# Last attention: first query slot alone, query low parts ahead of a weight's, three output slots side by side

## The chip, the core and the metric

The kernel runs on one core of a Trainium2 chip. The metric is the device time of one execution in microseconds (us), from the first to the last instruction with what lies around them; the median of several executions is given, and a profiled execution has its own time. All work is in fp32 that is split in two parts, as told below.

## The reference, cut to what matters

Four layers work on x of 512 tokens by 1024 features. The first three (a gated short convolution with forgetting attention, a conformer convolution module, and an HGRN2 recurrence, each followed by a feed-forward network) are not touched. The fourth, called d in the kernel, is attention in a sliding window with a sink, and its feed-forward network:

```
k, v = split(rms_norm(h, kv_norm) @ w_kv)            # 2 key/value heads of 64, shared by 8 query heads each
q = rms_norm(h, attn_norm) @ w_q                     # 16 query heads of 64
scores = q . k * 64**-0.5 - slope[head] * dist       # each block of 128 queries sees its own and the previous 128 keys
scores = where(0 <= dist < 128 and key exists, scores, -inf)
m = max(max(scores), sink); e = exp(scores - m)
probs = e / (sum(e) + exp(sink - m))
h = h + (probs @ v) @ w_o
h = h + conv_ffn(rms_norm(h, ffn_norm))
```

## The kernel before

**Layout.** Activations are feature-major: 8 chunks (KC = 8) of 128 features on the partitions, by 512 tokens. `h` is the residual. Each matmul operand x is kept as a high part in fp32r (`u_hi`, `w_hi`, `dcat_hi`), rounded by a copy on ScalarE, and a low part (`u_lo`, `w_lo`, `dcat_lo`), the difference, made on VectorE. A `product` is three matmuls of 512 columns: high by high, high by low, low by high. The engines' programs are written out by hand, each one in order, with semaphores between them; nothing reorders them.

**Weights.** All weights stand in one list of slots, each 128 x 1024 (512 KB). A slot makes one output chunk of 128 features: 8 products, k = 0 to 7, over the 8 input chunks. In layer d the slots are d_kv (2), d_q (8), d_out (8), then the feed-forward's. There is a ring of 4 places (RING) for a slot's raw, high and low parts. SyncE loads slot s into its place when slot s - 4 is over (`slot_done`). ScalarE makes the high part of slot s + 3 in `slot_over(s)` (AHEAD = 3), after slot s is over, and VectorE the low part of slot s + 3 in `low_over(s)`, which only waits for the high part. `w_ready` counts low parts in slot order; TensorE waits for it ahead of a slot.

**The norm.** The norm's factor is a root over the sum of squares per token (`rs`): TensorE sums with a matmul of ones (`mean_square`), ScalarE makes it with Ln and Exp (`root`), and it is multiplied in after the product, when a bank is evacuated. The gain is multiplied in ahead of it: ScalarE writes u_hi (`scaled_input`), VectorE u_lo (`scaled_low`).

**Layer d, in the order before.** TensorE: both d_kv slots side by side, the sum of squares, the first two query slots side by side (`two_chunks`, it waits for both weights), transposes of the values, scores of chunk 0, query slot 2. Then, for chunk c = 0 to 5 (a chunk is two query heads): scores of c + 1 (`window_scores`), probabilities times values of c - 1 (`window_values`), six of the eight products of query slot c + 3, transposes of the probabilities of c (`window_transpose`), and the last two products of that slot. After the loop d_out begins with two slots side by side (`out_chunks`); `window_ready` puts the transposes and values of chunks 6 and 7 among their products, and each k waits for `dol_ready`, the low part of attention output chunk k.

VectorE, per chunk c: `window_add` (distance bias, 8 instructions, line 2268) for c + 1, `window_probs` (sum, reciprocal, 8 multiplications, lines 2289 to 2297) for c, `low_over(d_q + c + 2)` (line 1626), `query_low(c + 2)` (two instructions on 64 partitions, line 2245), `window_max` (4 reductions, line 2278, then three small ones, the last of which releases ScalarE) for c + 1, `window_low(c - 1)` (line 2301) and `query_evac(c + 3)` (line 2238).

ScalarE, per chunk c: `window_out(c - 1)` (line 1576), four copies of transposed probabilities `dpt` (line 1585), `window_exp(c + 1)` (line 1563, 8 exponentials with their sums), `slot_over(d_q + c + 3)` (line 1092) and `query_high(c + 3)` (line 1550).

In PSUM the queries use banks 0 and 1, the values of chunk c bank 2 + c % 2, the scores and transposes banks 4 to 7. `add_over` on ScalarE and `add_out` on VectorE follow the output slots: one adds bank n % 4 to h, both then make the next inputs and the weight three slots on.

Of the kernel before, what the change touches and what calls it, by code (L numbers as in the profile page):

```python
# [5 lines left out]
F32 = mybir.dt.float32  # L6
# [9 lines left out]
KC = D // P  # L16
# [14 lines left out]
AHEAD = 3  # L31
HALF = FC // 2
FQ_BANKS = (0, 1, 2, 3, 6, 7)
HEAD_AT = (1, 3, 5, 6)

PHASES = 4
# [106 lines left out]
def build(nc, weights, vectors, squares, select_d, masks_d, x_t, out_t):  # L143
    with ExitStack() as ctx:
# [155 lines left out]
        def window_bank(n, e):  # L300

            return bank[4 + 2 * e + n // 2][:, 2 * WINDOW * (n % 2):2 * WINDOW * (n % 2 + 1)]

        def by_phase(x):

# [147 lines left out]
        def _(pe):  # L453
# [26 lines left out]
            def two_chunks(s, outs, xh, xl, ready, ready_hi=None):  # L480

                pe.wait_ge(w_ready, s + 2)
                for k in range(KC):
                    if k == 0 and ready_hi:
                        ready_hi()
                        for w in (w_hi, w_lo):
                            for e in range(2):
                                pe.matmul(outs[e][:, :], weight(w, (s + e) % RING, 0), xh[:, 0, :], start=w is w_hi, stop=False)
                        ready(0)
                        for e in range(2):  # L490
                            pe.matmul(outs[e][:, :], weight(w_hi, (s + e) % RING, 0), xl[:, 0, :], start=False, stop=False)
                        continue
                    ready(k)
                    for e in range(2):
                        j = (s + e) % RING
                        last = product(outs[e][:, :], weight(w_hi, j, k), weight(w_lo, j, k), xh[:, k, :], xl[:, k, :],
                                       k == 0, k == KC - 1)
                        if k == KC - 1:
                            last.then_inc(slot_done, 1)
# [33 lines left out]
            def normed_input(name):  # L533
                return lambda k: pe.wait_ge(u_ready, SPLIT[name] + k + 1)
# [491 lines left out]
            def window_values(c):  # L1026
                kv = c // 4
                if c >= 2:
                    pe.wait_ge(dol_ready, c - 1)
                o = bank[2 + c % 2]  # L1030
                for n in range(TT):
                    pe.wait_ge(dpt_ready, 4 * c + n + 1)
                    first = 0 if n else 1
                    for kt in range(first, 2):
                        for e in range(2):
                            last = pe.matmul(o[64 * e:64 * e + 64, n * P:(n + 1) * P],
                                             dv[:, n - 1 + kt, 64 * kv:64 * kv + 64],
                                             dpt[:, n, (2 * kt + e) * P:(2 * kt + e + 1) * P],
                                             start=(kt == first), stop=(kt == 1))
                last.then_inc(do_ready, 1)  # L1040

            def query_slot(n, ks):
                if n >= 4 and not ks[0]:
                    pe.wait_ge(d_q_evac, n - 1)
                chunk(SLOT["d_q"] + n, 0, bank[n % 2][:, :], u_hi, u_lo, ks=ks)

            two_chunks(SLOT["d_q"], bank[2:4], u_hi, u_lo, normed_input("d_q"), high_input("d_q"))
            pe.wait_ge(d_kv_evac, 2)
            for t in range(TT):
                last = pe.transpose(bank[0][:, t * P:(t + 1) * P], ut[:, 1, t * P:(t + 1) * P], ident)  # L1050
            last.then_inc(d_vt_full, 1)
            pe.wait_ge(d_kv_ready, 5)
            pe.wait_ge(dk_low, 6)
            window_scores(0)
            query_slot(2, range(KC))
            for c in range(KC - 2):
                window_scores(c + 1)
                if c:
                    window_values(c - 1)

                if c + 3 < KC:
                    query_slot(c + 3, range(KC - 2))
                window_transpose(c)
                if c + 3 < KC:
                    query_slot(c + 3, range(KC - 2, KC))
            window_scores(KC - 1)
            window_values(KC - 3)

            def window_ready(k):

                if k in (2, 5):
                    window_transpose(KC - 2 if k == 2 else KC - 1)
                elif k in (3, 6):
                    window_values(KC - 2 if k == 3 else KC - 1)
                pe.wait_ge(dol_ready, k + 1)

            out_chunks("d_out", dcat_hi, dcat_lo, added("d_mix"), window_ready)
            feed_forward("d")
            final_sums(1)

# [2 lines left out]
        def _(act):  # L1083
# [435 lines left out]
            def add_over(l):  # L1519

                for n in range(KC):
                    slot_over(SLOT[f"{l}_out"] + n)
                    scaled_input(f"{l}_fpre", f"{l}_mix", (n,))
                    square_h(f"{l}_fpre", f"{l}_mix", (n,))

# [9 lines left out]
            act.dma_start(dist[:, :], squares[:, 2 * P:]).then_inc(dist_landed, 16)  # L1535
            slot_over(SLOT["d_kv"])
            act.wait_ge(slot_done, SLOT["d_kv"] + 2)
            scaled_input("d_q", "c_ffn")
            slot_over(SLOT["d_kv"] + 1)
            root("d_pre")  # L1540
            act.wait_ge(d_kv_evac, 1)
            for kv in range(2):
                for e in range(2):
# [2 lines left out]
            def query_high(n):  # L1546

                act.wait_ge(d_q_evac, n + 1)
                for e in range(2):
                    act.activation(dq[rows_of(e), n % 2, e, :], ut[rows_of(e), n % 2, :], ACT.Copy).then_inc(dq_high, 1)  # L1550

            act.wait_ge(d_vt_full, 1)
            act.activation(dv[:, :, :], bank[0][:, :].rearrange("p (t n) -> p t n", t=TT), ACT.Copy).then_inc(d_kv_ready, 1)

# [8 lines left out]
                        act.activation(p, p, ACT.Exp, bias=nm[:, i:i + 1], accum_out=den[:, i:i + 1]).then_inc(ds_exp, 1)  # L1563

            query_high(0)
            query_high(1)
            slot_over(SLOT["d_q"])
            slot_over(SLOT["d_q"] + 1)
            window_exp(0)
            slot_over(SLOT["d_q"] + 2)  # L1570
# [2 lines left out]
            def window_out(c):  # L1573

                act.wait_ge(do_ready, c + 1)
                act.activation(dcat_hi[:, c, :], bank[2 + c % 2][:, :], ACT.Copy).then_inc(doh_ready, 1)

            for c in range(KC):
                if c:
                    window_out(c - 1)  # L1580
                for n in range(TT):
                    lo = 0 if n else 2 * P
                    act.wait_ge(dpt_full, 4 * c + n + 1)
                    after(act, do_ready, c)
                    act.activation(dpt[:, n, lo:], bank[4 + n][:, lo:], ACT.Copy).then_inc(dpt_ready, 1)
                if c + 1 < KC:
                    window_exp(c + 1)
                if c + 3 < KC:
                    slot_over(SLOT["d_q"] + c + 3)
                    query_high(c + 3)  # L1590
# [30 lines left out]
        def _(dve):  # L1621
# [100 lines left out]
            def add_out(l):  # L1722

                for n in range(KC + 1):
                    if n < KC:
                        dve.wait_ge(slot_done, SLOT[f"{l}_out"] + n + 1)
                        dve.tensor_tensor(h[:, n, :], h[:, n, :], bank[n % 4][:, :], ALU.add).then_inc(h_ready, 1)
                    if n:
                        scaled_low(f"{l}_fpre", n - 1)
                    if n >= 2:  # L1730
                        sum_squares(f"{l}_fpre", (n - 1,))
                    if n < KC:
                        low_over(SLOT[f"{l}_out"] + n)

            def add_ffn(l, stat, split):

# [471 lines left out]
            add_ffn("c", "d_pre", "d_kv")  # L2208


            low_over(SLOT["d_kv"])
            for c in range(KC):
                scaled_low("d_q", c)
            low_over(SLOT["d_kv"] + 1)
            for e in range(2):
                none = ones[rows_of(1 - e), 0:1].unsqueeze(2).to_broadcast([64, 2, T])
                dve.tensor_scalar(dk_lo[rows_of(1 - e), :, e, :], none, 0.0, None, ALU.mult).then_inc(dk_low, 1)
            dve.wait_ge(rs_ready, RS["d_pre"] + 1)
            for i in range(2):
                dve.tensor_tensor(ut[:, i, :], bank[i][:, :], rs[:, :], ALU.mult).then_inc(d_kv_evac, 1)  # L2220


            for kv in range(2):
                for e in range(2):
# [21 lines left out]
                                      dq[rows_of(e), n % 2, e, :].bitcast(F32), ALU.subtract).then_inc(dq_low, 1)  # L2246

            query_evac(0)
            query_evac(1)
            query_low(0)  # L2250
            query_low(1)
            low_over(SLOT["d_q"])
            low_over(SLOT["d_q"] + 1)
# [44 lines left out]

            def window_low(c):
                dve.wait_ge(doh_ready, c + 1)  # L2300
                dve.tensor_tensor(dcat_lo[:, c, :], bank[2 + c % 2][:, :], dcat_hi[:, c, :].bitcast(F32), ALU.subtract)\
                   .then_inc(dol_ready, 1)

            window_add(0)
# [2 lines left out]
            for c in range(KC):  # L2307
                if c + 1 < KC:
                    window_add(c + 1)
                window_probs(c)  # L2310
                if c + 2 < KC:
                    low_over(SLOT["d_q"] + c + 2)
                    query_low(c + 2)
                if c + 1 < KC:
                    window_max(c + 1)
                if c:
                    window_low(c - 1)
                if c + 3 < KC:
                    query_evac(c + 3)
            window_low(KC - 1)  # L2320
# [119 lines left out]
```

## Time and profile before

| | us |
|---|---|
| median of 3 runs | 2374.59 (2374.01 to 2375.52) |
| the profiled execution | 2376.0 |
| its span, first to last instruction | 2374.2 |
| TensorE matmuls busy | 2318.5 (98%) |
| TensorE weight loads busy | 1959.8 (83%) |
| VectorE busy | 1330.3 (56%) |
| ScalarE busy | 875.2 (37%) |
| DMA, mean over the span | 92 GB/s |
| granted TensorE clock, mean | 0.992 |

The profile is one execution on the chip. Its times count from the start of the span. PE is TensorE's matmul, PEld its weight load, DVE VectorE, ACT ScalarE, SPq SyncE's queue. "L461" is line 461 of the kernel. In a list of waits or a timeline, `<-` names what ended an idle time. Matmuls are pipelined: one of 512 columns is shown as 0.39 us long and the next begins 0.23 us after it, so their pace is read from their starts. A granted clock of 1.00 is 2.4 GHz, 0.50 is 1.2 GHz.

### The profile page before, as it was taken

To read this page: it belongs to the slowest core of one execution; us is meant where nothing else is said; L and a number is where in the kernel's file an instruction comes from. 1 tells how busy PE (TensorE), PEld (TensorE's weight loads), DVE (VectorE), ACT (ScalarE), POOL (GpSimd) and SP (SyncE) were. 2 spreads that over 40 slices of the span, in tenths; PEclk is the share of its full clock that TensorE was granted. 3 is DMA by queue.
4 is the path that set the end of the run, shared out by engine and by line. 5 is a ranking of instruction groups with operands and counts; after the bars stand their busy time and mean duration, and the time that the engine had idled before them with its cause. 6 is when DMAs were issued, how large, how long until landed. Compare 5 with 4: busy or idle time off the path is not lost.

```text
span 2374.2 us, 36384 instructions
## 1 busy us (share of the span) xinstructions
PE 2318.5 (98%) x14188; PEld 1959.8 (83%) x14188; DVE 1330.3 (56%) x1934; ACT 875.2 (37%) x1337; POOL 3.3 (0%) x5
## 2 busy tenths in 40 slices
PE   9999999999898999999999999999999989999998
PEld 7788888889887988888988877888888777888888
DVE  6564755522767565542366575666633885766523
ACT  6444422222524532222342364333322574333322
POOL 0000000000000000000000000000000000000000
PEclk9999999999998999999999999999999999999999
DMA  4122243222362233223232112323333202333322
GB/s 159 62 63 86 83 125 96 94 94 88 104 183 80 80 107 96 95 93 96 89 104 83 59 58 71 98 97 97 97 97 96 66 28 89 97 97 97 97 91 87
DMA packets 82604, 218.70 MB, mean 92 GB/s; under 512 B 10944, under 2 KB 31808, under 8 KB 82496
## 3 DMA queue, kind: packets, MB, share of 16 engines
q1 hardware_dynamic: 75600, 208.23, 27.9%
q10 hardware_dynamic: 6896, 8.92, 1.2%
q8 instruction: 81, 1.33, 0.2%
q14 instruction: 27, 0.22, 0.0%
HBM read 212.78 MB, written 4.34 MB: 91 GB/s over the span
## 4 chain that ended last, share of the span: by engine, by line
PE 83%; DVE 9%; ACT 5%; issue 2%; DMA 1%; SPq 0%; ACTq 0%; DVEq 0%
PE bank L461 24%; PE bank L463 23%; PE bank L462 23%; PE bank L657 2%; PE bank L656 2%; PE bank L658 2%; DVE w_lo L1626 1%; PE bank L815 1%; ACT w_hi L1092 1%; ACT ds L1563 1%; DVE m L1682 1%; DVE acc L1655 1%; DVE h L1687 1%; DVE small L2278 1%; DVE ds L2297 1%
## 5 line engine op out<-in xcount | busy, mean ns | idle before, releaser
L461 PE MATMUL bank<-u_hi,w_hi 128*128 128x512 f32 (+1 forms) x2090 | 797.0, 381 | 13.0 <-DVE w_lo L1626 6.4
L1092 ACT ACTIVATE w_hi<-raw 128x1024 fp32r<-128x1024 f32 x378 | 399.9, 1059 | 1080.8 <-PE bank L463 944.4
L463 PE MATMUL bank<-u_hi,w_lo 128*128 128x512 f32 (+1 forms) x2090 | 786.7, 376 | 0.0
L462 PE MATMUL bank<-u_lo,w_hi 128*128 128x512 f32 (+1 forms) x2090 | 786.6, 376 | 0.0
L1626 DVE TENSOR_TENSOR w_lo<-raw,w_hi 128x1024 fp32r<-128x1024 f32 x378 | 461.3, 1222 | 398.1 <-ACT w_hi L1092 397.6
L461 PEld LDWEIGHTS bank<-u_hi,w_hi 128*128 128x128 f32 x2090 | 393.4, 188 | 93.3 <-DVE w_lo L1626 6.6
L463 PEld LDWEIGHTS bank<-u_hi,w_lo 128*128 128x128 f32 x2090 | 393.3, 188 | 72.8
L462 PEld LDWEIGHTS bank<-u_lo,w_hi 128*128 128x128 f32 x2090 | 393.8, 188 | 70.9 <-issue 1.2
L461 PE MATMUL bank<-hid_hi,w_hi 128*128 (+1 forms) x440 | 173.4, 394 | 0.0
L463 PE MATMUL bank<-hid_hi,w_lo 128*128 (+1 forms) x440 | 172.5, 392 | 0.0
L462 PE MATMUL bank<-hid_lo,w_hi 128*128 (+1 forms) x440 | 170.8, 388 | 0.0
L656 PE MATMUL bank<-hid_hi,w_hi 128*128 128x256 f32 x528 | 147.9, 280 | 0.0
L657 PE MATMUL bank<-hid_lo,w_hi 128*128 128x256 f32 x528 | 147.7, 280 | 0.0
L1779 DVE TENSOR_TENSOR ut<-gconv,bank 128x512 f32<-128x512 f32 x88 | 60.5, 687 | 155.6 <-PE bank L463 148.1
L658 PE MATMUL bank<-hid_hi,w_lo 128*128 128x256 f32 x528 | 147.3, 279 | 0.0
L656 PEld LDWEIGHTS bank<-hid_hi,w_hi 128*128 128x128 f32 x528 | 99.3, 188 | 0.2
L657 PEld LDWEIGHTS bank<-hid_lo,w_hi 128*128 128x128 f32 x528 | 99.1, 188 | 0.2
L658 PEld LDWEIGHTS bank<-hid_hi,w_lo 128*128 128x128 f32 x528 | 98.8, 187 | 0.0
L463 PEld LDWEIGHTS bank<-hid_hi,w_lo 128*128 128x128 f32 x440 | 82.6, 188 | 19.4
L462 PEld LDWEIGHTS bank<-hid_lo,w_hi 128*128 128x128 f32 x440 | 82.6, 188 | 18.5
L1773 DVE SCALAR_TENSOR_TENSOR gconv<-ut,vec,gconv 128x511 f32<-128x511 f32 x88 | 66.0, 750 | 56.5 <-ACT gconv L1241 50.6
L461 PEld LDWEIGHTS bank<-hid_hi,w_hi 128*128 128x128 f32 x440 | 82.7, 188 | 16.5
(301 smaller groups left out, 2495.8 us busy)
## 6 DMA issues: line engine op xcount, KB each, us to landing
raw<-weights_dram SPq DMA_DIRECT2D x365, 512.0 KB, 3.5
bz<-gated_dram SPq DMA_DIRECT2D x32, 268.0 KB, 4.3
raw<-weights_dram ACTq DMA_DIRECT2D x13, 512.0 KB, 3.8
gated_dram<-bz SPq DMA_DIRECT2D x8, 274.0 KB, 3.0
h<-x_t_dram SPq DMA_DIRECT2D x8, 256.0 KB, 6.3
out_dram<-m SPq DMA_DIRECT2D x4, 256.0 KB, 2.4
out_dram<-m ACTq DMA_DIRECT2D x4, 256.0 KB, 2.5
cmask<-masks_dram ACTq DMA_DIRECT2D x4, 224.0 KB, 3.9
```

The source lines that it names most:

```text
L461: pe.matmul(out, wh, xh, start=start, stop=False)
L462: pe.matmul(out, wh, xl, start=False, stop=False)
L463: return pe.matmul(out, wl, xh, start=False, stop=stop)
L656: pe.matmul(out, wh, xh, start=first, stop=False, skip_group_check=True)
L657: pe.matmul(out, wh, xl, start=False, stop=False, skip_group_check=True)
L658: return pe.matmul(out, wl, xh, start=False, stop=final, skip_group_check=True)
L815: last = pe.matmul(out[32 * g:32 * g + 32, i * COLS:(i + 1) * COLS], bw[:, b, TILES * i + g, q, :], bz4[:, b, TILES * i + g, at:at + COLS] ...
L1092: act.activation(w_hi[:, j, :], raw[:, j, :], ACT.Copy).then_inc(hi_ready, 1)
L1563: act.activation(p, p, ACT.Exp, bias=nm[:, i:i + 1], accum_out=den[:, i:i + 1]).then_inc(ds_exp, 1)
L1626: dve.tensor_tensor(w_lo[:, j, :], raw[:, j, :], w_hi[:, j, :].bitcast(F32), ALU.subtract).then_inc(w_ready, 1)
L1773: dve.scalar_tensor_tensor(out=gconv[:, b, back:], in0=ut[:, b, 0:T - back], scalar=w, in1=gconv[:, b, back:], op0=ALU.mult, op1=ALU.add). ...
L1779: dve.tensor_tensor(ut[:, b, :], gconv[:, b, :], bank[2 * b + 1][:, :], ALU.mult).then_inc(ht_ready, 1)
```

## The change

It edits layer d alone, on three engines, in three parts.

1. **First query slot alone.** TensorE runs d_q's slot 0 alone (bank 2), then the values' transposes, then slot 1 (bank 3), then the scores of chunk 0. ScalarE makes u_hi 0 and 1, then the root, then u_hi 2 to 7, and puts the high part of the third query weight behind the keys' high parts. VectorE sets the zero halves of `dk_lo` first, evacuates keys and values after u_lo 3, makes the second query weight's low part after u_lo 5, and `query_low(0)` and a weight's low part ahead of `query_evac(1)`.
2. **Query's low parts ahead of a weight's.** In VectorE's loop `query_low(c + 2)` stands ahead of `low_over(d_q + c + 2)`.
3. **Three output slots side by side.** `out_part(k)` is the product k of d_out's slots 0, 1 and 2, in banks 0, 1 and 3. Parts 0 and 1 stand in the loop's turn c = 5 ahead of the transposes of chunk 5; parts 2 to 7 stand among transposes and values of chunks 6 and 7. Each part waits for `dol_ready`, for all query evacuations and for the low part of d_out's third weight. Slot 3 (bank 2) does its products 0 and 1 ahead of part 7 and the others behind it. The values of chunks 4 to 6 use bank 2 and those of chunk 7 bank 4, so `window_values` waits for one more `window_low` from chunk 5 on. The high and low part of d_out's fourth weight move into the loops, and `add_over` and `add_out` take the weights in the order of `OUT_NEXT`.

```diff
+OUT_NEXT = {"c": tuple(range(KC)), "d": (1, 2, None) + tuple(range(3, KC))}
+OUT_BANKS = {"c": (0, 1, 2, 3), "d": (0, 1, 3, 2)}
...
+        def value_bank(c):
+            return bank[2 + c % 2 if c < KC // 2 else 2 if c < KC - 1 else 4]
...
             def window_values(c):
                 kv = c // 4
                 if c >= 2:
-                    pe.wait_ge(dol_ready, c - 1)
-                o = bank[2 + c % 2]
+                    pe.wait_ge(dol_ready, c if c > KC // 2 else c - 1)
+                o = value_bank(c)
...
+            def out_part(k):
+                pe.wait_ge(dol_ready, max(k + 1, 4))
+                pe.wait_ge(d_q_evac, KC)
+                pe.wait_ge(w_ready, SLOT["d_out"] + 3)
+                for n in range(3):
+                    j = (SLOT["d_out"] + n) % RING
+                    last = product(bank[OUT_BANKS["d"][n]][:, :], weight(w_hi, j, k), weight(w_lo, j, k),
+                                   dcat_hi[:, k, :], dcat_lo[:, k, :], k == 0, k == KC - 1)
+                    if k == KC - 1:
+                        last.then_inc(slot_done, 1)
...
-            two_chunks(SLOT["d_q"], bank[2:4], u_hi, u_lo, normed_input("d_q"), high_input("d_q"))
+            chunk(SLOT["d_q"], 0, bank[2][:, :], u_hi, u_lo, normed_input("d_q"))
             pe.wait_ge(d_kv_evac, 2)
             for t in range(TT):
                 last = pe.transpose(bank[0][:, t * P:(t + 1) * P], ut[:, 1, t * P:(t + 1) * P], ident)
             last.then_inc(d_vt_full, 1)
+            chunk(SLOT["d_q"] + 1, 0, bank[3][:, :], u_hi, u_lo)
...
                 if c + 3 < KC:
                     query_slot(c + 3, range(KC - 2))
+                else:
+                    out_part(0)
+                    out_part(1)
                 window_transpose(c)
...
             window_values(KC - 3)
-            out_chunks("d_out", dcat_hi, dcat_lo, added("d_mix"), window_ready)
+            out_part(2)
+            out_part(3)
+            window_transpose(KC - 2)
+            out_part(4)
+            window_values(KC - 2)
+            out_part(5)
+            window_transpose(KC - 1)
+            out_part(6)
+            window_values(KC - 1)
+            chunk(SLOT["d_out"] + 3, 0, bank[OUT_BANKS["d"][3]][:, :], dcat_hi, dcat_lo, ks=range(2))
+            out_part(7)
+            chunk(SLOT["d_out"] + 3, 0, bank[OUT_BANKS["d"][3]][:, :], dcat_hi, dcat_lo, ks=range(2, KC))
+            for n in range(4, KC):
+                added("d_mix")(n)
+                chunk(SLOT["d_out"] + n, 0, bank[OUT_BANKS["d"][n % 4]][:, :], dcat_hi, dcat_lo)
...
# ScalarE
-            scaled_input("d_q", "c_ffn")
-            slot_over(SLOT["d_kv"] + 1)
+            scaled_input("d_q", "c_ffn", range(2))
             root("d_pre")
+            scaled_input("d_q", "c_ffn", range(2, KC))
...
+            slot_over(SLOT["d_kv"] + 1)
             act.wait_ge(d_vt_full, 1)
...
             query_high(0)
+            slot_over(SLOT["d_q"])
             query_high(1)
-            slot_over(SLOT["d_q"])
...
+                if c == KC - 2:
+                    act.wait_ge(slot_done, SLOT["d_out"])
+                    high_part(SLOT["d_out"] + AHEAD)
...
# VectorE
-            low_over(SLOT["d_kv"])
-            for c in range(KC):
-                scaled_low("d_q", c)
-            low_over(SLOT["d_kv"] + 1)
+            dve.wait_ge(slot_done, SLOT["d_kv"])
             for e in range(2):
                 none = ones[rows_of(1 - e), 0:1].unsqueeze(2).to_broadcast([64, 2, T])
                 dve.tensor_scalar(dk_lo[rows_of(1 - e), :, e, :], none, 0.0, None, ALU.mult).then_inc(dk_low, 1)
-            dve.wait_ge(rs_ready, RS["d_pre"] + 1)
-            for i in range(2):
-                dve.tensor_tensor(ut[:, i, :], bank[i][:, :], rs[:, :], ALU.mult).then_inc(d_kv_evac, 1)
+            for c in range(KC):
+                scaled_low("d_q", c)
+                if c == 3:
+                    dve.wait_ge(rs_ready, RS["d_pre"] + 1)
+                    for i in range(2):
+                        dve.tensor_tensor(ut[:, i, :], bank[i][:, :], rs[:, :], ALU.mult).then_inc(d_kv_evac, 1)
+                if c == 5:
+                    low_over(SLOT["d_kv"])
...
             query_evac(0)
+            query_low(0)
+            low_over(SLOT["d_kv"] + 1)
             query_evac(1)
-            query_low(0)
             query_low(1)
...
                 if c + 2 < KC:
+                    query_low(c + 2)
                     low_over(SLOT["d_q"] + c + 2)
-                    query_low(c + 2)
...
+                if c == KC - 1:
+                    low_part(SLOT["d_out"] + AHEAD)
```

## Rows read from the trace of the kernel before

**Rows 1.** The page, chain that ended last, by engine and by line.

```profile
PE 83%; DVE 9%; ACT 5%; issue 2%; DMA 1%; SPq 0%; ACTq 0%; DVEq 0%
```

**Rows 2.** Waits of TensorE, 1848 to 1966: in total, times, longest.

```profile
PE bank L1012 <- DVE dq L2245: 6.8, 6, 3.9
```

**Rows 3.** Busy time by engine (instructions) in a stretch, then granted clock and DMA.

```profile
1865.20:1870.60 5.40, 5.33 (x21) 4.97 (x22) 5.17 (x10) 2.45 (x3) 0.00 (x0) 0.50 0.00 0
1907.45:1919.29 11.84, 11.31 (x82) 9.30 (x82) 11.12 (x31) 8.38 (x25) 0.00 (x0) 1.00 0.14 46
1938.80:1942.30 3.50, 3.26 (x14) 2.71 (x14) 3.44 (x9) 3.09 (x7) 0.00 (x0) 0.51 0.00 0
```

**Rows 4.** The chain in order of time, 1845 to 1966: start, us, what.

```profile
1876.27 1.85 DVE ds L2268 x7
...
1919.27 2.21 DVE small L2278 x4
1922.18 0.82 ACT ds L1563 x5
...
1926.45 2.06 DVE ds L2297 x8
1928.51 1.13 DVE w_lo L1626
```

**Rows 5.** Timeline of VectorE, 1847 to 1870: start, length, instruction, idle before.

```profile
1848.45 1.23 DVE L1626 TENSOR_TENSOR w_lo<-raw,w_hi 128x1024 fp32r<-128x1024 f32 x1 [4.64 <-ACT w_hi L1092]
1849.59 5.38 DVE L1660 SCALAR_TENSOR_TENSOR u_lo<-h,vec,u_hi 128x512 fp32r<-128x512 f32 x8
...
1862.33 1.29 DVE L2238 SCALAR_TENSOR_TENSOR ut<-bank,rs 128x512 f32<-128x512 f32 x2
1863.72 2.84 DVE L2245 TENSOR_TENSOR dq<-ut,dq 64x512 fp32r<-64x512 f32 x4
...
1869.04 1.14 DVE L2268 SCALAR_TENSOR_TENSOR ds<-dist,bank 128x128 f32<-128x128 f32 x4
```

**Rows 6.** Timeline of ScalarE, 1847 to 1879.

```profile
1847.36 1.06 ACT L1092 ACTIVATE w_hi<-raw 128x1024 fp32r<-128x1024 f32 x1 [4.81 <-PE bank L463]
1848.32 5.00 ACT L1133 ACTIVATE u_hi<-h,vec 128x512 fp32r<-128x512 f32 x8
...
1854.18 0.67 ACT L1114 ACTIVATE rs<-bank,eps 128x512 f32<-128x512 f32 x1
...
1863.06 2.59 ACT L1550 ACTIVATE dq<-ut 64x512 fp32r<-64x512 f32 x4 [1.03 <-DVE ut L2238]
...
1877.96 1.05 ACT L1092 ACTIVATE w_hi<-raw 128x1024 fp32r<-128x1024 f32 x1
```

**Rows 7.** Timeline of VectorE, 1932 to 1942: the low part of d_out's third weight.

```profile
1940.25 1.22 DVE L1626 TENSOR_TENSOR w_lo<-raw,w_hi 128x1024 fp32r<-128x1024 f32 x1
```

**Rows 8.** Timeline of TensorE, from three stretches between 1880 and 2001.

```profile
1881.14 1.69 PE L1022 MATMUL bank<-identity,ds 128*128 128x128 f32 x14
1882.58 0.48 PE L461 MATMUL bank<-u_hi,w_hi 128*128 128x512 f32 x1
...
1938.91 3.26 PE L1022 MATMUL bank<-identity,ds 128*128 128x128 f32 x14 [3.96 <-DVE ds L2297]
1942.96 0.33 PE L1012 MATMUL bank<-dk_hi,dq 128*128 128x128 f32 x1 [0.80 <-DVE dq L2245]
...
1945.02 1.75 PE L1036 MATMUL bank<-dpt,dv 128*64 128x128 f32 x28
...
2000.67 0.61 PE L488 MATMUL bank<-u_hi,w_hi 128*128 128x512 f32 x2
```

**Rows 9.** Busy time of TensorE alone, clock and DMA, while only output slots run.

```profile
1965.10:2000.60 35.50, 35.50 (x158) 1.00 0.33 104
```

**Rows 10.** Timeline of ScalarE, 1965 to 1974, as d_out's first two slots end.

```profile
1967.53 1.06 ACT L1092 ACTIVATE w_hi<-raw 128x1024 fp32r<-128x1024 f32 x1 [1.78 <-PE bank L463]
...
1971.43 1.06 ACT L1092 ACTIVATE w_hi<-raw 128x1024 fp32r<-128x1024 f32 x1 [1.71 <-DMA raw<-weights_dram]
```

More of the change, by code:

```diff
@@ L1067, in _ @@
             window_values(KC - 3)
[L1069 to L1075, printed above, removed]
-            out_chunks("d_out", dcat_hi, dcat_lo, added("d_mix"), window_ready)
+            out_part(2)
[13 more added lines that the diff above has]
+                chunk(SLOT["d_out"] + n, 0, bank[OUT_BANKS["d"][n % 4]][:, :], dcat_hi, dcat_lo)
             feed_forward("d")
@@ L1521, in add_over @@
                 for n in range(KC):
-                    slot_over(SLOT[f"{l}_out"] + n)
+                    if OUT_NEXT[l][n] is not None:
+                        slot_over(SLOT[f"{l}_out"] + OUT_NEXT[l][n])
                     scaled_input(f"{l}_fpre", f"{l}_mix", (n,))
@@ L1575, in window_out @@
                 act.wait_ge(do_ready, c + 1)
-                act.activation(dcat_hi[:, c, :], bank[2 + c % 2][:, :], ACT.Copy).then_inc(doh_ready, 1)
+                act.activation(dcat_hi[:, c, :], value_bank(c)[:, :], ACT.Copy).then_inc(doh_ready, 1)
             for c in range(KC):
@@ L1726, in add_out @@
                         dve.wait_ge(slot_done, SLOT[f"{l}_out"] + n + 1)
-                        dve.tensor_tensor(h[:, n, :], h[:, n, :], bank[n % 4][:, :], ALU.add).then_inc(h_ready, 1)
+                        dve.tensor_tensor(h[:, n, :], h[:, n, :], bank[OUT_BANKS[l][n % 4]][:, :], ALU.add).then_inc(h_ready, 1)
                     if n:
@@ L1731, in add_out @@
                         sum_squares(f"{l}_fpre", (n - 1,))
-                    if n < KC:
-                        low_over(SLOT[f"{l}_out"] + n)
+                    if n < KC and OUT_NEXT[l][n] is not None:
+                        low_over(SLOT[f"{l}_out"] + OUT_NEXT[l][n])
             def add_ffn(l, stat, split):
@@ L2300, in window_low @@
                 dve.wait_ge(doh_ready, c + 1)
-                dve.tensor_tensor(dcat_lo[:, c, :], bank[2 + c % 2][:, :], dcat_hi[:, c, :].bitcast(F32), ALU.subtract)\
+                dve.tensor_tensor(dcat_lo[:, c, :], value_bank(c)[:, :], dcat_hi[:, c, :].bitcast(F32), ALU.subtract)\
                    .then_inc(dol_ready, 1)
```

## Prediction

> **What bounds the kernel now.** I read the page's chain that ended last first: 83% of it is TensorE, 9% VectorE and 5% ScalarE [rows 1], so nearly everywhere the time is the sum of TensorE's matmuls, and an edit counts by the TensorE idle time it removes or adds. The change only touches the last attention, from 1847 us (the last key/value product) to 2000.67 us, where the next stage's products begin [rows 8]. The matmuls before and after are the same in number, so the question is where TensorE waits in there. In this trace it waits for the query's low parts (6.8 us in six waits, longest 3.9) [rows 2], for the probabilities before transposes (3.96 us at 1938.91) [rows 8], and runs at 1.2 GHz after each of these two long waits: granted clock 0.50 over 1865.20 to 1870.60, 0.51 over 1938.80 to 1942.30 [rows 3].
>
> Who is late there is the second question, and the chain in order of time answers it [rows 4]: from 1876 us on it does not run through TensorE. One turn of the loop over the eight chunks is: window_max on VectorE (2.21 and three small operations, 1919.27 to 1921.94), eight exponentials on ScalarE (to 1925.91), window_probs on VectorE (2.06, to 1928.51), a weight's low part (1.13) and two query low parts (0.71 each by the x4 row of [rows 5]), and then window_max again at 1931.1. That adds up to the period of 11.84 us. In one such stretch TensorE is busy 11.31 us and VectorE 11.12 [rows 3]; both look full, but the loop is closed over VectorE and ScalarE. TensorE's wait of about half a microsecond per turn is slack, it is not the price.
>
> **Part 1, the first query slot alone, the root sooner.** It removes the 3.9 us wait before the first scores [rows 2, 8]: the second query slot, 24 matmuls, is what TensorE does meanwhile. What is late next is VectorE, so I walk its queue in its new order with the old durations [rows 5, 6].
> - The key/value slots are over at 1847.4 (ScalarE's first row). VectorE now sets the two zeros at once (0.72 each), in what was its idle 4.64 us. Gain 1.4 us.
> - u_hi of chunks 0 and 1 end near 1849.0 and 1849.7; then Ln (0.70) and Exp (0.63) stand in ScalarE's queue before u_hi 2, which ends near 1851.5. VectorE's u_lo 0 and 1 (0.66 each, 5.38 for eight) are done at 1850.4, so it waits 1.2 us.
> - u_lo 2, 3 to 1852.9; the two evacuations of keys and values (1.2, as the x2 row) to 1854.1; u_lo 4, 5 to 1855.5; a weight's low part (1.15) to 1856.6; u_lo 6, 7 to 1858.0; four key low parts (2.85) to 1860.8.
> - The query's evacuation, its high part on ScalarE and its low part are a round trip: from 1862.33 to 1863.72 in the old trace, 1.39 us, of which 0.7 is VectorE waiting. Before, the second evacuation stood in that hole. Now low parts 0 run 1862.3 to 1863.7, a weight's low part to 1864.9, evacuation 1 at 1865.1, low parts 1 from 1866.5 to 1867.9 (a second hole of 0.7), two weights' low parts to 1870.2.
> So window_add(0) starts at 1870.2, against 1869.04: 1.2 later. TensorE: the first slot is fed by u_lo, ends at about 1858.8, transposes, second slot to 1864.9, scores(0) at once. In the old kernel the turn after that was itself late: window_add(1) began only at 1876.27, because scores(1) stood behind half-clock matmuls, and ended at 1878.7; the exponentials of chunk 0, for which window_probs behind it waits as well, were done by 1878.0, where ScalarE's next weight begins [rows 3, 4, 6]. That cost 0.6, and it goes. Net: the chain runs 0.6 us later than before (bounds: 0 if one hole closes, 2 if ScalarE's queue adds one more weight's high part of 1.06).
>
> **Part 2, query low parts ahead of the weight's low part.** The same three operations in another order, on the engine that closes the loop: TensorE's waits for dq go, the turn stays 11.84 us. Worth 0 on the path; the cover is the chain itself. It has a price at one place, next.
>
> **Part 3, output slots 0, 1, 2 side by side.** out_part(0) and (1) stand in TensorE's queue ahead of window_transpose(5). They wait for w_ready of d_out's third slot. Its low part is low_over(d_q + 7), which VectorE makes in turn c = 5, after window_probs(5): at 1940.25, 1.22 long, in the old trace [rows 7]. In the new order it comes 0.6 later by part 1 and 1.43 later by part 2 (two query low parts now stand before it): 1942.3 to 1943.5. TensorE has finished values(4) near 1934.6 and is idle for some 9 us, where it was idle 3.96. Queued behind that wait is window_transpose(5), which before began at 1938.91; for it wait ScalarE's copies of chunk 5 and, in its queue behind them, the exponentials of chunk 6. So the cover of the late weight is gone and the softmax chain itself is moved back.
>
> From 1943.5 on TensorE has work nearly without a hole, so its sum is the time. Durations from [rows 8, 9]: matmuls of 512 columns 35.50/158 = 0.225 (0.227 with the start-to-start of the stretch's ends); transposes of a chunk 1882.58 - 1881.14 = 1.44; scores 1945.02 - 1942.96 = 2.06; values 1.7.
> - eight output slots, 192 matmuls: 43.6
> - three chunks of transposes 4.3, scores(7) 2.1, three chunks of values 5.1
> - scores(7) waits for ScalarE's four copies of chunk 5: 1.0. Three small waits later, for window_low and for the last probabilities: 0.8 in all.
> - The fourth-next weight. Three slots now end together, so d_out's fifth weight can be loaded only then. In the old trace two slots were over by 1967.53; the high part of the weight that could only be loaded then began at 1971.43, after the DMA, and high and low part take 1.06 and 1.23: 6.2 us to 1973.7 [rows 10]. Slot 0 ends two products (1.4) before slot 2, and TensorE has six products (4.1) of slot 3 left: wait 6.2 - 1.4 - 4.1 = 0.7; three loads in a row may stretch the first, so 0.9 (bounds 0.7 to 2).
> Sum 57.8. End at full clock: 1943.5 + 57.8 = 2001.3, against 2000.67: +0.6.
> - The clock. A 9 us wait is longer than both after which this trace shows 1.2 GHz. Old stretches at half clock lasted 3.5 and 5.4 us after work began [rows 3]; what runs in them takes twice as long, so 1.75 to 2.7 us; now it falls on out_part(0) and (1), with nothing to hide it. Before, both fell on stretches that waited for VectorE anyway. I take 2.2 (bounds 0 and 4.1, the whole of the 18 matmuls).
> On what brings the clock back: in this trace it was 2.4 GHz again after 3.26 us of transposes alone [rows 3, 8]. The Trainium skill ("TensorE: Matmul & The Clock Gate", Part 4) says that transposes do not count as busy in the same way as matmuls do; by it the new order, which resumes with dense matmuls, would regain the clock sooner than the old and cost nearer 0 than 2.2, a total of +0.6. The row does not bear it out.
>
> Sum: +0.6 + 2.2 = +2.8 us. Against the profiled execution's own 2376.0 us (span 2374.2) that is 2378.8; the median of the shown runs is 1.4 lower, so **2377.4 us**. Below about 0.2% (4.7 us) a measurement of this kernel can't tell a difference from none, and this forecast lies inside it.
>
> **Rivals.**
> A. TensorE's waits are the price. Then the first wait gives back its 3.9 less the 1.3 that u_lo's pace costs, the other five waits for dq 2.9, the two half-clock stretches 2.5, and the wait of 3.96 is filled by out_part(0): about -10, 2364. For it: TensorE 98% busy, and 11.31 of 11.84 in a turn. Against: the chain [rows 4] has no TensorE in it. The Trainium skill ("Perfetto Trace Analysis", Optimization Strategy) tells to look for the gaps of the engine one improves and to make what ends them start sooner; followed for TensorE, that is this rival. Chance 0.08.
> B. The third weight is not late, or the wait hurts less than I think (the low part of d_out + 2 is ready near 1938, the clock stays). The chain still ends with transposes of chunk 7, at 1959.9 + 0.6, and behind them stand values, 8 products of the side-by-side and fourth slot, its rest and four slots, 36 us: 1997 to 1998, so -3 us, 2372. Chance 0.17.
> C. Slower by over 4.7 us: the first slot's matmuls come in pairs with holes of about 1.2 us, six matmuls in 2.5 us. If that is too little and the clock falls there, the second query slot takes up to twice its 5.45 us, evacuation 1 and the first window_add come 3 to 5 later, and this is pure loss on the chain: +6 to +8, 2381 to 2383. It decides from about 2 us of half clock ahead of 1865 on; or the same total comes when half clock covers all of out_part(0) and (1) and the fifth weight is 2 late. For: the trace has two falls in this stage. Against: both followed waits of 3.9 and more. Chance 0.27.
> The forecast itself: 0.48.
>
> **How the numbers follow.** Likeliest is +2.8; its own range is +0.6 to +4.9. B pulls the low end to 2371, C the high end to 2383. Faster by over 0.2%: A, and a little of B: 0.10. Slower by over 0.2%: C and the upper end of the forecast: 0.32. Within: 0.58.
>
> **What would show it.** No wait of TensorE for dq ahead of the first scores; window_add(0) about 1 us later than 1869.0; turns still 11.8 us long; one TensorE wait of 8 to 9 us released by w_lo (L1626's subtraction), near 1935 to 1943.5, and window_transpose(5) some 9 us later than before, with granted clock 0.5 behind it. A turn shorter than 11.6 us, or output parts that begin before 1940, would make the prediction wrong.

## The result and the profile after

The change made the kernel slower: 2380.64 us median of 12 runs against 2375.87 of 12 of before, a ratio of 1.0021 with a 95% interval of 1.0012 to 1.0030, that is 2.9 to 7.1 us. The forecast was +2.8 us, and 2377.4 us for the median. The profiled execution of the changed kernel took 2379.3 us (span 2377.5), 3.3 more than 2376.0.

Since the change touches one stage, I compare that stage inside the profiles. "The stage" runs from the start of ScalarE's first high part behind the key/value slots (1847.36 before [rows 6], 1847.10 after) to the start of the next stage's products (2000.67 in [rows 8], 2004.02 after): 153.31 us before, **156.92 us after, +3.6**. Its two ends in the profile after:

```profile
1847.10 1.06 ACT L1119 ACTIVATE w_hi<-raw 128x1024 fp32r<-128x1024 f32 x1 [4.81 <-PE bank L469]
2004.02 0.62 PE L494 MATMUL bank<-u_hi,w_hi 128*128 128x512 f32 x2
```

From there to the last instruction it is 373.5 us in both. The medians differ by 1.2 more than the stage does; that is inside the interval, and I don't explain it.

What TensorE waits for in the stage after the change (total, times, longest), which answers to [rows 2]. Lines have moved: L467 is an output or query product, L1018 the scores, L1028 the transposes.

```profile
PE bank L467 <- DVE w_lo L1658: 8.9, 1, 8.9
PE bank L467 <- DVE u_lo L1692: 3.5, 4, 1.1
PE bank L1028 <- DVE ds L2331: 2.7, 5, 1.4
PE bank L1018 <- ACT dpt L1614: 0.9, 1, 0.9
PE bank L1018 <- DVE ds L2302: 0.4, 1, 0.4
```

The waits for dq are all gone. One wait of 8.9 us for a weight's low part stands there now. Here it is in TensorE's timeline, with the 18 matmuls of output parts 0 and 1 and the transposes of chunk 5 behind it:

```profile
1932.84 1.75 PE L1042 MATMUL bank<-dpt,dv 128*64 128x128 f32 x28
1943.45 0.77 PE L467 MATMUL bank<-dcat_hi,w_hi 128*128 128x512 f32 x1 [8.87 <-DVE w_lo L1658]
1944.02 0.63 PE L468 MATMUL bank<-dcat_lo,w_hi 128*128 128x512 f32 x1
...
1948.95 1.69 PE L1028 MATMUL bank<-identity,ds 128*128 128x128 f32 x14
1951.53 0.30 PE L1018 MATMUL bank<-dk_hi,dq 128*128 128x128 f32 x1 [0.88 <-ACT dpt L1614]
```

The transposes that began at 1938.91 before [rows 8] begin at 1948.95. VectorE's timeline shows where the awaited weight stands in its queue, behind probabilities and query low parts (it answers to [rows 7]):

```profile
1938.56 2.06 DVE L2331 TENSOR_SCALAR ds<-ds,small 128x128 f32<-128x128 f32 x8
1940.65 1.40 DVE L2278 TENSOR_TENSOR dq<-ut,dq 64x512 fp32r<-64x512 f32 x2
1942.08 1.22 DVE L1658 TENSOR_TENSOR w_lo<-raw,w_hi 128x1024 fp32r<-128x1024 f32 x1
```

Busy time by engine and granted clock in three stretches (they answer to [rows 3]; the columns are PE, PEld, DVE, ACT, POOL, clock, DMA share, GB/s): a turn of the loop, the half-clock stretch, and output parts 0 and 1.

```profile
1907.12:1918.96 11.84, 11.53 (x84) 9.23 (x83) 11.11 (x31) 8.37 (x25) 0.00 (x0) 1.00 0.15 46
1939.40:1946.20 6.80, 2.75 (x7) 2.20 (x8) 6.64 (x16) 1.31 (x3) 0.00 (x0) 0.50 0.00 0
1943.40:1948.95 5.55, 5.50 (x18) 4.40 (x19) 3.02 (x8) 0.00 (x0) 0.00 (x0) 0.74 0.00 0
```

The turn is still 11.84 us: TensorE is a little busier in it (11.53 for 11.31), VectorE as before (11.11 for 11.12). The clock fell in the long wait, and the half clock covered the first 2.75 us of the output parts.

### The profile page after: what moved, and what is told of

Its sections match the earlier page's. It is cut to its first block, busy times and chain, and to the rows that moved or that the text cites. A ratio compares the mean times of both kernels' runs of the same rounds, so it can differ in the third digit from the quotient of the medians.

```text
span 2377.5 us, 36391 instructions
## 1 busy us (share of the span) xinstructions
PE 2314.2 (97%) x14188; PEld 1952.7 (82%) x14188; DVE 1330.1 (56%) x1934; ACT 874.6 (37%) x1337; POOL 3.3 (0%) x5
## 3 DMA queue, kind: packets, MB, share of 16 engines
q8 instruction: 81, 1.33, 0.2%
## 4 chain that ended last, share of the span: by engine, by line
PE 82%; DVE 9%; ACT 5%; issue 2%; DMA 1%; SPq 1%; ACTq 0%; DVEq 0%
PE bank L467 23%; PE bank L469 23%; PE bank L468 23%; PE bank L663 2%; PE bank L662 2%; PE bank L664 2%; DVE w_lo L1658 2%; ACT w_hi L1119 1%; PE bank L821 1%; DMA raw<-weights_dram 1%; DVE m L1714 1%; DVE acc L1687 1%; ACT ds L1592 1%; DVE h L1719 1%; DVE small L2312 1%
## 5 line engine op out<-in xcount | busy, mean ns | idle before, releaser
L467 PE MATMUL bank<-u_hi,w_hi 128*128 128x512 f32 (+1 forms) x2092 | 798.0, 381 | 18.2 <-DVE w_lo L1658 7.1
L467 PEld LDWEIGHTS bank<-u_hi,w_hi 128*128 128x128 f32 x2092 | 393.8, 188 | 101.1 <-DVE w_lo L1658 8.4
L467 PE MATMUL bank<-hid_hi,w_hi 128*128 (+1 forms) x440 | 173.4, 394 | 0.0
L467 PEld LDWEIGHTS bank<-hid_hi,w_hi 128*128 128x128 f32 x440 | 82.7, 188 | 16.5
```

Of the source, the lines that this page charges most:

```text
L467: pe.matmul(out, wh, xh, start=start, stop=False)
```

## The experiments

Ten kernels were run, each beside the kernel before on the same chip. The totals have intervals of 2 to 3 us to either side, so the steps are read from the stage's length in each profile, as defined above; it was 153.31 us before and 156.92 us with the change. Each length comes from one profiled execution. How much such a reading scatters can be seen at two places: the first window_add came 21.67 or 21.68 us into the stage in all five kernels with the old head and 22.66 to 22.68 us in all seven with the new one, while a wait that a load ends, for the fifth output weight, lay between 0.9 and 1.5 us in the eight kernels with part 3. So steps of a few tenths behind that load are not read as effects of an edit.

### Each part alone

**e1, part 1 alone.** The edit is the change's own, on TensorE, ScalarE and VectorE ahead of the loop; output and loop as before.

```diff
-            two_chunks(SLOT["d_q"], bank[2:4], u_hi, u_lo, normed_input("d_q"), high_input("d_q"))
+            chunk(SLOT["d_q"], 0, bank[2][:, :], u_hi, u_lo, normed_input("d_q"))
...
+            chunk(SLOT["d_q"] + 1, 0, bank[3][:, :], u_hi, u_lo)
```

> The kernel before with part 1 alone: first query slot alone, root sooner, the queue orders of ScalarE and VectorE that go with it. The stage's length is counted from the first high part after the key/value slots (before 1847.36) to the start of the next stage's products (before 2000.67): 153.3 us before, 156.9 with the whole change. Theory (the softmax loop over VectorE and ScalarE sets the pace): the wait of 3.9 ahead of the first scores is gone, the first window_add is about 1.0 later, turns stay 11.84, stage 153.8, total +0.5 us (0 to +1.2). Rival A (TensorE's waits are the price): the wait's 3.9 less what the first slot loses to u_lo, and 2.5 of half clock, come off: stage 149, total -4.

Measured: stage 153.85 us (+0.5), total 0.9998 of before (0.9989 to 1.0007). The first window_add came 22.66 us into the stage, against 21.68. Turns 11.84. TensorE's waits:

```profile
PE bank L1022 <- DVE ds L2301: 6.3, 3, 4.0
PE bank L1012 <- DVE dq L2248: 3.7, 6, 1.1
PE bank L461 <- DVE u_lo L1662: 3.5, 4, 1.1
```

The 3.9 us wait is gone and nothing is won: 3.5 us came back as waits for u_lo, and the first window_add, which VectorE makes, came 1.0 later. Half of that was won back in the first turn, as forecast. Rival A's 149 is refuted for this part.

**e2, part 2 alone.**

```diff
-                    low_over(SLOT["d_q"] + c + 2)
                     query_low(c + 2)
+                    low_over(SLOT["d_q"] + c + 2)
```

> The kernel before with part 2 alone: query_low(c + 2) ahead of low_over in VectorE's loop. Theory: TensorE's waits for dq inside the loop go and come back as waits for probabilities; turns 11.84 as before, stage 153.3, total 0 (-0.3 to +0.3). Rival A: the five waits of 2.9 in all come off: stage 150.4, total -2.9.

Measured: stage 153.31 us, to the hundredth that of before; total 1.0001 (0.9992 to 1.0010); turns 11.85. TensorE's waits:

```profile
PE bank L1022 <- DVE ds L2297: 7.5, 6, 4.6
PE bank L1012 <- DVE dq L2245: 3.9, 1, 3.9
```

The kernel before had this beside its waits for dq [rows 2]:

```profile
PE bank L1022 <- DVE ds L2297: 6.0, 3, 4.0
```

The five waits for dq inside the loop have gone, and six waits for probabilities stand there where three did. The stage is as long as it was, so TensorE idles as long as before, in other places. This is the cleanest reading of the study: these waits of TensorE in the loop are slack.

**e3, part 3 alone.** The change with parts 1 and 2 undone.

> The kernel before with part 3 alone: three output slots side by side, parts 0 and 1 ahead of the transposes of chunk 5. Theory: VectorE's low part of the third output weight is 1.4 earlier than with part 2 and 0.5 to 1 earlier than with part 1, so out_part(0) begins near 1941.5; a TensorE wait of 7 us; the rest as in the whole change, so the stage is 155.0 and the total +1.7 (+0.5 to +2.5). Rival A: filling TensorE's waits pays: stage 150, total -3.

Measured: stage 155.23 us (+1.9), total 1.0010 (1.0001 to 1.0019). TensorE waited 6.7 us for the third output weight, and the 18 matmuls of parts 0 and 1 took 6.02 us at a granted clock of 0.67:

```profile
PE bank L467 <- DVE w_lo L1656: 6.7, 1, 6.7
```

```profile
1940.18:1946.20 6.02, 6.02 (x19) 4.74 (x19) 4.46 (x10) 0.00 (x0) 0.00 (x0) 0.67 0.00 0
```

Part 3 is where the loss is. Parts 1 and 2, worth +0.5 and 0.0 alone, add 1.7 on top of it: they put the third weight's low part later, which only costs where output parts wait for it. Parts 0 and 1 begin 94.13 us into the stage here (1940.17 less 1846.04) and 96.35 with the change, 2.2 later. The half clock took 0.5 more here (6.02 us for 5.50), and that leaves the 1.7.

### The wait for the third output weight

**e4, output parts behind the transposes.** The whole change but for this:

```diff
-                else:
-                    out_part(0)
-                    out_part(1)
                 window_transpose(c)
                 if c + 3 < KC:
                     query_slot(c + 3, range(KC - 2, KC))
+                else:
+                    out_part(0)
+                    out_part(1)
```

> The whole change, but in the turn c = 5 out_part(0) and (1) stand behind window_transpose(5) instead of ahead of it. Theory: what hurts is that the transposes of chunk 5, and with them the copies, the exponentials of chunk 6 and all that follows, are queued behind the wait for the third output weight. Now transposes begin near 1939.5, out_part(0) still near 1943.5, a wait of 2 instead of 9, the half clock falls mostly on transposes: stage 153.9 to 154.4 (2.5 to 3 less than 156.9), total +0.6 to +1.1 against before. Rival (the price is in the two extra slots' worth of weights or elsewhere, not in the order): stage stays at 156 to 157.

Measured: stage 153.08 us, 3.8 less than the whole change; total 1.0004 of before (0.9995 to 1.0013). It was 0.8 better than the lower end of what I had expected. The half clock lay on the transposes alone and the parts ran at full pace (4.18 us).

```profile
PE bank L1028 <- DVE ds L2331: 7.2, 6, 4.6
PE bank L467 <- DVE u_lo L1692: 3.5, 4, 1.1
PE bank L467 <- DVE w_lo L1658: 1.0, 1, 1.0
```

The parts began 96.35 us into the stage in both kernels, so when they begin is not what makes the difference. Of the 3.8 us, 1.3 is the clock (4.18 for 5.50). The rest is what was queued behind them: in the changed kernel the transposes of chunk 5 (1.4 us) and the wait of 0.9 for ScalarE's copies come after the parts, and here they don't.

**e10, the third weight early.** The whole change, with the high part of d_out's third weight moved ahead of ScalarE's exponentials in turn 4, and its low part to the end of VectorE's turn 4.

```diff
# ScalarE
+                if c == 4:
+                    act.wait_ge(slot_done, SLOT["d_q"] + c + 3)
+                    high_part(SLOT["d_out"] + 2)
                 if c + 1 < KC:
                     window_exp(c + 1)
...
-                    slot_over(SLOT["d_q"] + c + 3)
+                    if c != 4:
+                        slot_over(SLOT["d_q"] + c + 3)
...
# VectorE
-                    low_over(SLOT["d_q"] + c + 2)
+                    if c != 5:
+                        low_over(SLOT["d_q"] + c + 2)
...
                     query_evac(c + 3)
+                if c == 4:
+                    low_part(SLOT["d_out"] + 2)
```

> The whole change, with one thing moved: ScalarE makes the high part of d_out's third weight in turn 4 ahead of the exponentials of chunk 5 instead of behind them, and VectorE its low part at the end of turn 4 instead of in turn 5 behind the probabilities. The other weights stay where they are, so turns 1 to 4 stay 11.84. Theory (the whole loss of part 3 comes from that one low part): out_part(0) begins near 1936.7 at the latest, TensorE waits 2 us instead of 9, the transposes of chunk 5 begin near 1941, no half clock; stage 150.4 against 156.9 (-6.5) and 153.3 before (-2.9). This is rival B of the prediction, made true. Rival (part 3 loses by the fifth weight, by the waits on bank 2 or by its longer queue instead): stage 154 or more.

Measured: stage 149.65 us, 7.3 less than the whole change and 3.7 less than before; total 0.9989 (0.9980 to 0.9998). Parts 0 and 1 took 4.17 us at full clock, behind a wait of 1.9 us:

```profile
PE bank L1028 <- DVE ds L2335: 2.7, 5, 1.4
PE bank L467 <- DVE w_lo L1662: 1.9, 1, 1.9
```

```profile
1935.20:1937.30 2.10, 0.18 (x4) 0.00 (x0) 2.10 (x5) 2.10 (x11) 0.00 (x0) 1.00 0.00 0
1937.33:1941.50 4.17, 4.17 (x18) 3.41 (x19) 4.10 (x17) 3.24 (x10) 0.00 (x0) 1.00 0.00 0
```

The whole loss of part 3 comes from one weight's low part, an operation of 1.2 us that stood behind the probabilities in VectorE's queue; its high part had to move with it. It also makes up 0.6 of what lies below my 150.4: the last turn is now 11.26, since its weight's low part had gone to where VectorE works while ScalarE makes the exponentials.

### The clock

**e5, TensorE kept awake.** The whole change, with matmuls of ones in the wait.

```diff
                 else:
+                    pe.wait_ge(d_q_evac, KC)
+                    keep_awake(bank[0], 68)
                     out_part(0)
                     out_part(1)
```

> The whole change, with 68 matmuls of ones by ones (128 columns, into bank 0, which the first output part overwrites) in TensorE's queue ahead of out_part(0), where it waits 9 us for the third output weight. In this kernel such a matmul takes about 0.12 us (L457's pace), so they last 8 us, are over before the weight is there, and only keep the clock up. Theory: the parts 0 and 1 run at 2.4 GHz, 18 matmuls in 4.1 us instead of 5.5; stage 155.5 against 156.9, total 1.4 us less than with the change (+2 to +3.4 against before). Rival (half clock is no price here): stage 156.9, no change.

Measured: stage 162.55 us, total 1.0039 (1.0025 to 1.0053). The size was wrong: such a matmul is two rows of 0.112 us, not one, so they held the parts back by 7.1 us (103.41 us into the stage for 96.35; the 6.9 in the expectation of e9 is a little short) and the sum says nothing. But parts 0 and 1 then took 4.18 us at clock 1.00.

**e9, the same with 36.**

> As e5, with 36 matmuls of ones instead of 68. In e5's trace each one is two rows of 0.112 us, so 68 of them lasted 15.2 us, held out_part(0) back by 6.9 us and made the sum useless; but its parts 0 and 1 ran at 2.4 GHz, 4.18 us for 18 matmuls against 5.50. 36 last 8.1 us, from 1934.8 to 1942.9, and are over before the third weight is there (1943.4). Theory: stage 155.5 to 155.6 against 156.9, 1.3 us less than the whole change. Rival (the half clock is no price, because something else holds the parts back by as much): 156.9.

Measured: stage 155.11 us, 1.8 less than the whole change (1.3 expected); total 1.0015 (1.0006 to 1.0024). The matmuls of ones, then the parts:

```profile
1934.46:1942.61 8.15, 8.15 (x73) 8.15 (x73) 7.50 (x22) 5.41 (x16) 0.00 (x0) 1.00 0.00 0
1942.61:1946.77 4.16, 4.16 (x20) 3.41 (x19) 2.97 (x8) 0.00 (x0) 0.00 (x0) 1.00 0.00 0
```

The parts began at the same place in the stage (96.37 for 96.35) and took 4.16 us instead of 5.50. So the half clock costs 1.3 us at this place. The transposes of chunk 5 show the same 1.3: they began 100.53 us into the stage, against 101.85 with the change. The other 0.5 of the 1.8 arose at the fifth weight, for which TensorE waited 0.9 us here and 1.33 in the changed kernel. That wait was 1.2 to 1.5 in the six other kernels with part 3, so e9 is the odd one; I don't ascribe it to the edit. The 1.3 rests on one execution of each kernel.

### What the loop is worth

**e6, a weight's low part in the shadow of the exponentials.** The kernel before, with part 2 and this:

```diff
                     query_low(c + 2)
-                    low_over(SLOT["d_q"] + c + 2)
...
                     query_evac(c + 3)
+                if c + 2 < KC:
+                    low_over(SLOT["d_q"] + c + 2)
```

> The kernel before with part 2's order, and a turn's weight low part (low_over(d_q + c + 2), 1.14 us) moved to the end of VectorE's turn, behind query_evac. There VectorE works while ScalarE makes the exponentials, and had 0.5 us to spare. Theory (the loop over VectorE and ScalarE sets the pace): a turn is max 2.6, then the longer of exponentials 3.95 and VectorE's own work in their shadow (0.6 + 0.6 + 1.14 + 2.4 = 4.7), then probabilities 2.4 and query low parts 1.4: 11.2 instead of 11.84, six turns, stage 149.5 against 153.3, total -3.8. Rival A (TensorE sets the pace, 11.3 busy in a turn): 11.84 less 0.5 at most if its waits for dq went with part 2 alone, which e2 says they don't; so turns 11.84 and 0.

Measured: stage 148.87 us, 4.4 less than before (3.8 expected); total 0.9986 (0.9977 to 0.9995); turns 11.26, one of 10.72. One turn in the chain in order of time (start, us, what), which answers to [rows 4]:

```profile
1902.16 2.21 DVE small L2278 x4
...
1905.36 0.68 DVE ut L2238
1906.03 1.13 DVE w_lo L1626
1907.17 1.70 DVE ds L2268 x6
...
1909.90 2.06 DVE ds L2297 x8
1912.00 0.69 DVE dq L2245
```

ScalarE has left the chain. In [rows 4] the exponentials stood between L2278 and L2297; now VectorE's own work stands there, and VectorE alone closes the loop. Rival A had 0 here.

**e7, all weights of the loop one turn earlier, with parts 2 and 3.** ScalarE makes the high part ahead of the exponentials, in time that it waited for the maxima; VectorE makes the low part behind query_evac. Against e3 with part 2:

```diff
# ScalarE
+                if c + 3 < KC:
+                    act.wait_ge(slot_done, SLOT["d_q"] + c + 3)
+                    high_part(SLOT["d_q"] + c + 3 + AHEAD)
                 if c + 1 < KC:
                     window_exp(c + 1)
...
-                    slot_over(SLOT["d_q"] + c + 3)
...
# VectorE
                     query_low(c + 2)
-                    low_over(SLOT["d_q"] + c + 2)
+                    if c == 0:
+                        low_over(SLOT["d_q"] + 2)
...
                     query_evac(c + 3)
+                    low_over(SLOT["d_q"] + c + 3)
```

> Part 3 (output parts ahead of the transposes) and part 2, with head as before, and the weights one turn earlier: ScalarE makes the high part of the slot ahead of the exponentials, in its idle time, and VectorE the low part behind query_evac, so d_out's third weight is there near 1935. Theory: out_part(0) and (1) fill TensorE's wait ahead of the transposes of chunk 5, no clock fall there, turns of 11.2 to 11.4, later parts fill the waits of chunks 6 and 7; stage 146.5 (145 to 148) against 153.3, total -6.8 us. If only the late third weight were cured and turns stayed at 11.84 (rival B of the prediction), stage 150.5, total -3. Rival A gives the same sign and can't be told apart here but by the turn's length.

Measured: stage 146.38 us, **6.9 less than before**; total 2368.8 us, 0.9974 (0.9964 to 0.9985). TensorE's waits:

```profile
PE bank L1018 <- DVE dq L2277: 3.9, 1, 3.9
PE bank L467 <- DVE w_lo L1658: 1.0, 1, 1.0
```

**e8, the same with part 1.** The edit of e7, made to the whole change.

> The whole change with the weights one turn earlier as in the run before: its difference to that run is part 1 alone. Theory: part 1 makes the first window_add 1.0 later and saves 0.5 of it in the first turn, and keeps the clock up ahead of it; stage 147.0 to 147.5, total -6 us. Rival (part 1 pays once the late weight is out of the way): stage 144 or less.

Measured: stage 146.84 us, 0.5 more than e7, while its TensorE has no 3.9 us wait; total 2369.42 us, 0.9975 (0.9964 to 0.9986). Part 1 doesn't pay with the late weight cured either. Both kernels beat the one before and the changed one.

## Why the prediction was right, step by step

- **What bounds the stage.** The loop over VectorE and ScalarE does. e2 shows it by removing TensorE's waits at no gain, e6 by shortening VectorE's and ScalarE's way and gaining.
- **Part 1.** The walk through VectorE's queue gave the first window_add 1.2 us later; it was 0.99 later in the stage (22.67 against 21.68), with both holes of 0.7 us. Net +0.6 on the chain was forecast, +0.5 measured (e1). The clock didn't fall there (1.00 in the row of the first query slot below).

```profile
1861.92 1.40 DVE L2278 TENSOR_TENSOR dq<-ut,dq 64x512 fp32r<-64x512 f32 x2 [0.70 <-ACT dq L1578]
1866.06 1.40 DVE L2278 TENSOR_TENSOR dq<-ut,dq 64x512 fp32r<-64x512 f32 x2 [0.70 <-ACT dq L1578]
1869.77 0.48 DVE L2302 SCALAR_TENSOR_TENSOR ds<-dist,bank 128x128 f32<-128x128 f32 x2
```

- **Part 2.** Forecast 0; e2 has 0.00 in the stage. Turns 11.84 as said.
- **Part 3, the wait.** Out_part(0) forecast at 1943.5, measured 1943.45, which counted from the start of the stage is 0.2 later than forecast (96.35 for 96.14); a wait of some 9 us, measured 8.87; transposes of chunk 5 at 1948.95, ten later than before.
- **The sum behind it.** 57.8 us at full clock plus 2.2 for the clock, 60.0 in all; measured 2004.02 - 1943.45 = 60.6. Three terms were mis-sized and partly cancel. The clock costs 1.3, not 2.2 (e9 against the change: 4.16 for 5.50), because it came back 2.75 us into the work. The prediction's other price, near 0 because dense matmuls would bring the clock back sooner than transposes do, isn't borne out: the half clock lasted 2.75 us of dense matmuls with the change, some 3.9 in e3, and 3.3 us of transposes alone in the kernel before. The wait for the fifth weight was 1.33, not 0.9:

```profile
1979.67 1.06 ACT L1119 ACTIVATE w_hi<-raw 128x1024 fp32r<-128x1024 f32 x1 [6.06 <-DMA raw<-weights_dram]
1982.14 0.47 PE L467 MATMUL bank<-dcat_hi,w_hi 128*128 128x512 f32 x1 [1.33 <-DVE w_lo L1658]
```

  The high part began 4.1 us after the load was issued (1975.53). The prediction's guess that three loads in a row may stretch the first agrees with the runs: from the issue to that high part it took 3.5 to 3.8 us in the four kernels where two slots end together (before: 1967.67 to 1971.43; e1, e2, e6), and 4.0 to 4.3 us in seven of the eight with three; only e9 had 3.7 (1973.34 to 1977.04). The stretch is then about 0.4 here, where I had put 0.2. Why e9 escaped it is not shown, nor did a run vary the loads alone. Beside these, the 192 matmuls took, without what the half clock added, 44.7 us where I had 43.6 (0.227 each), since those that stand in short groups between transposes and values take more on average: a group of nine took 2.23 us, 1960.91 to 1963.14. Added up: +1.1 for the pace, -0.9 for the clock, +0.4 for the fifth weight make the +0.6; the rest of the sum (transposes, scores, values and the small waits) came out within 0.1 as a whole. With the 0.2 by which the parts began later in the stage, that is the step from the forecast 2.8 to the measured 3.6. That the total came so near owes something to luck: the pace and the clock were each off by about 1 us, in opposite directions.
- **Size.** +2.8 forecast, +3.6 in the stage, +4.8 between medians with an interval of 2.9 to 7.1. The sign was right. But the median's difference lies just above the 4.7 us that I had called the bound of what can be told from nothing, and so in the class to which I gave a chance of 0.32, not in the one with 0.58.
- **Two sums that don't come out.** The terms of rival A (3.9 less 1.3, 2.9, 2.5 and 3.96) add up to 12, not to about 10. The range's upper end by its own terms is 0.6 + 4.1 = 4.7, not 4.9. Neither bears on the forecast.
- **Rival A** fell with e1 and e2. **Rival B** didn't happen, since TensorE waited 8.9 us for that weight; e10 made its condition true and gained 3.7, of which 0.6 is the shorter last turn, where I had said 3. **Rival C's** clock fall in the first query slot did not come.

## What to carry to other kernels

Before filling an engine's idle time, ask whether that idle time is on the path: follow the chain through one turn of the loop and add up its pieces, and if they make the period without the engine, its waits are slack, and taking them away moves them elsewhere. Work put into a hole must have all its inputs when the hole opens; if one of them comes from the queue of the very engine that closes the loop, the filler waits with the loop, and all that stands behind the filler waits too. The gain then lay in the other engine's queue: one operation moved to where VectorE was idle gained 4.4 us (e6, with part 2, which alone is worth 0.0), where the three edits together lost 3.6.

## What was unexpected of the hardware

- A stretch in which TensorE works only part of the time can keep its full clock. In the changed kernel's first query slot it waits 1.1 us ahead of this stretch and three times inside it, there 2.9 us in all beyond the pace of back-to-back matmuls, and the clock stays at 1.00:

```profile
1849.70:1858.54 8.84, 6.41 (x24) 4.17 (x25) 7.76 (x12) 8.05 (x13) 0.00 (x0) 1.00 0.20 79
```

  The waits of 3.9, 6.7 and 8.9 us in one piece were each followed by 1.2 GHz, those of 1.9 and 1.0 us (e10, e7) were not.
- The half clock covered 5.4 us of work after the 3.9 us wait of before, some 3.9 us after the 6.7 us wait of e3 and 2.75 us after the 8.9 us wait of after: its price didn't grow with the wait. It was 1.3 us in the change and 1.9 in e3 (6.02 us for 4.17).
- A 128-column fp32 matmul of ones is two rows of 0.112 us, 0.224 in all (e5: 68 of them in 15.21 us).
- Where three weight loads are issued close together, the first one's weight was usable later than where two are: 4.0 to 4.3 us from the first issue to the high part made of it in seven of eight kernels, against 3.5 to 3.8 in four.
